# z and the mixing products of layer 0 feature-major, with upper and lower parts of the tokens in one 512-column product

## What is computed

```python
D_MODEL = 1024; SEQ = 256; D_INNER = 2048; POOL_WINDOWS = (2, 4, 8, 16)

def pool_layer(x, norm_g, w_in, w_pool, pool_scale, w_out):
    h = rms_norm(x, norm_g)
    u, z = jnp.split(h @ w_in, 2, axis=-1)
    # pool_mixer: mean over the last 2, 4, 8 or 16 tokens less u itself, by
    # group of 512 features; then per group  mixed = pooled @ w_pool[g]
    y = pool_mixer(u, w_pool, pool_scale) * jax.nn.silu(z)
    return x + y @ w_out
```

## Time and profile before

| | |
|---|---|
| median of three runs | 431.68 us |
| the profiled execution | 431.68 us, its span 429.9 us |
| TensorE busy | 423.5 us, 99% |
| VectorE, ScalarE, GpSimd busy | 281.4, 231.0, 163.1 us |
| loads | 73.8 MB read; a granule of 1 MB lands 5.0 to 5.5 us after its issue |
| granted TensorE clock | 1.00 throughout |

### The profile page before, as it was taken

How to read it: one execution, slowest core, us unless ns; L and a number is a source line. 1 busy time by engine, 2 the same in 40 slices (tenths; PEclk the granted TensorE clock), 3 DMA queues, 4 the chain that set the end, 5 groups by cost and what they waited for, 6 DMA issues and landing times.

```text
span 429.9 us, 5672 instructions
## 1 busy us (share of the span) xinstructions
PE 423.5 (99%) x2214; PEld 362.7 (84%) x2214; DVE 281.4 (65%) x340; ACT 231.0 (54%) x406; POOL 163.1 (38%) x111
## 2 busy tenths in 40 slices
PE   8999999999999999999999999999999999999997
PEld 8979898988888888888788888888888888888885
DVE  3866898688985544356664798447983579836532
ACT  5745545444554443578447765477654786546310
POOL 0077417267000000089804595055940559300000
PEclk9999999999999999999999999999999999999999
DMA  8987578645455747436833667236672355731002
GB/s 273 386 285 272 195 244 314 214 159 178 167 197 175 217 137 221 123 94 204 295 101 99 186 184 226 91 100 193 196 216 84 99 191 196 246 105 41 2 0 98
DMA packets 38026, 75.25 MB, mean 175 GB/s; under 512 B 1648, under 2 KB 1776, under 8 KB 38000
## 3 DMA queue, kind: packets, MB, share of 16 engines
q1 hardware_dynamic: 37280, 73.83, 52.8%
q10 hardware_dynamic: 720, 1.07, 0.8%
HBM read 73.84 MB, written 1.05 MB: 174 GB/s over the span
## 4 chain that ended last, share of the span: by engine, by line
PE 85%; POOL 7%; DMA 2%; DVE 2%; ACT 1%; SPq 1%; issue 1%; DVEq 0%
PE acc L599 23%; PE acc L601 22%; PE acc L600 22%; PE aux L654 4%; POOL wide L344 3%; PE acc L644 3%; PE acc L643 3%; PE acc L641 3%; DMA raw<-in_w_in_dram 2%; PE aux L738 2%; POOL k_s L337 1%; PE aux L745 1%; SPq L232 1%; PE aux L757 1%; PE aux L756 1%; PE aux L755 1%
## 5 line engine op out<-in xcount | busy, mean ns | idle before, releaser
L836 DVE TENSOR_TENSOR w_lo<-raw,w_hi 128x2048 fp32r<-128x2048 f32 x65 | 165.2, 2548 | 57.6 <-ACT w_hi L367 57.5
L367 ACT ACTIVATE w_hi<-raw 128x2048 fp32r<-128x2048 f32 x64 | 121.9, 1915 | 28.3 <-PE acc L601 21.7
L599 PE MATMUL acc<-w_hi,hT_hi 128*128 128x512 f32 x320 | 127.7, 399 | 1.0 <-DVE w_lo L836 1.0
L601 PE MATMUL acc<-w_hi,hT_lo 128*128 128x512 f32 x320 | 124.9, 390 | 0.0
L600 PE MATMUL acc<-w_lo,hT_hi 128*128 128x512 f32 x320 | 124.6, 389 | 0.0
L601 PEld LDWEIGHTS acc<-w_hi,hT_lo 128*128 128x128 f32 x320 | 60.1, 188 | 13.0
L599 PEld LDWEIGHTS acc<-w_hi,hT_hi 128*128 128x128 f32 x320 | 60.2, 188 | 12.9 <-DVE w_lo L836 1.4
L600 PEld LDWEIGHTS acc<-w_lo,hT_hi 128*128 128x128 f32 x320 | 60.2, 188 | 11.5
L599 PE MATMUL acc<-w_hi,aT_hi 128*128 128x512 f32 x160 | 63.7, 398 | 0.0
L601 PE MATMUL acc<-w_hi,aT_lo 128*128 128x512 f32 x160 | 62.4, 390 | 0.0
L600 PE MATMUL acc<-w_lo,aT_hi 128*128 128x512 f32 x160 | 62.3, 389 | 0.0
(11 more groups left out here) (125 smaller groups left out, 593.7 us busy)
## 6 DMA issues: line engine op xcount, KB each, us to landing
raw<-in_w_in_dram SPq DMA_DIRECT2D x46, 1024.0 KB, 5.5
raw<-in_w_out_dram SPq DMA_DIRECT2D x16, 1024.0 KB, 5.0
raw<-in_w_pool_dram SPq DMA_DIRECT2D x4, 1024.0 KB, 5.5
raw<-in_w_in_dram SPq DMA_DIRECT2D x8, 256.0 KB, 7.4
wide<-in_xT_dram ACTq DMA_DIRECT2D x4, 256.0 KB, 6.6
xs<-in_x_dram SPq DMA_DIRECT2D x1, 1024.0 KB, 7.7
out_dram<-ysb SPq DMA_DIRECT2D x4, 256.0 KB, 2.0
wide<-in_table_dram SPq DMA_DIRECT2D x1, 256.0 KB, 8.9
```

The lines of the kernel that those rows point to most:

```text
L367: act.activation(w_hi[:, slot, :], raw[:, slot, :], ACT.Copy).then_inc(hi_made, 1)
L599: pe.matmul(a, shi, whi, start=first and k == 0, stop=False)
L601: ins = pe.matmul(a, slo, whi, start=False, stop=last and k == GK - 1)
L836: dve.tensor_tensor(w_lo[:, slot, :], raw[:, slot, :], w_hi[:, slot, :].bitcast(F32), ALU.subtract).then_inc(w_split, 1)
```

## The change

z and the mixing products become feature-major. The upper and lower parts of the tokens lie side by side (`hT`, `aT`), so a tile of `tile_of_two` is two products: w_lo with the upper part (256 columns), then w_hi with both (512 columns). The left half of the bank then holds two of the three terms and the right half the third; all four tiles of a granule take a bank each (`quad`). ScalarE copies the right halves of two banks to SBUF, VectorE adds the left halves. For z, VectorE also multiplies by the token's factor (in the free dimension now), ScalarE takes tanh from SBUF, VectorE makes the gate. For y0, VectorE multiplies by the channel's scale and the gate, ScalarE and VectorE split the result from SBUF. The transposes of y0 are gone. Mixing granules alternate between `quad[0]` and `quad[1]`. The wait for `tables_made` moves from ScalarE to VectorE. The diff, cut to layer 0 (semaphore declarations and the shifted counts of layer 1 are left out):

```diff
@@ -98,21 +98,20 @@
-        hT_hi = sb("hT_hi", [P, KD, SEQ], F32R)
-        hT_lo = sb("hT_lo", [P, KD, SEQ], F32R)
-        aT_hi = sb("aT_hi", [P, KI, SEQ], F32R)
-        aT_lo = sb("aT_lo", [P, KI, SEQ], F32R)
+        hT = sb("hT", [P, KD, 2, SEQ], F32R)
+        aT = sb("aT", [P, KI, 2, SEQ], F32R)
...
+        rstd_half_b = sb("rstd_half_b", [P, SEQ])
+        second = sb("second", [P, 2 * SEQ])
...
+        probs_pair = sb("probs_pair", [P, 6 * P])
...
+        hT_hi, hT_lo = hT[:, :, 0, :], hT[:, :, 1, :]
+        aT_hi, aT_lo = aT[:, :, 0, :], aT[:, :, 1, :]
+        probs, probsT = probs_pair[:, 0:3 * P], probs_pair[:, 3 * P:]
+        lo_part = [t.rearrange("p (f s) -> p f s", f=2) for t in (probs_pair[:, 0:2 * SEQ], second[:, :])]
+        gateT = wide[:, :, :].rearrange("p t n -> p (t n)").rearrange("p (f s) -> p f s", f=KI)
+        y0 = [ysb[:, b].rearrange("p t n -> p (t n)").rearrange("p (f s) -> p f s", f=HPG) for b in range(2)]
...
-        acc = [[ctx.enter_context(nc.psum_tensor(f"acc{b}{t}", [P, COLS], F32)) for t in range(TT)] for b in range(2)]
-        aux = [ctx.enter_context(nc.psum_tensor(f"aux{i}", [P, COLS], F32)) for i in range(4)]
+        quad = [ctx.enter_context(nc.psum_tensor(f"quad{b}", [P, 4, COLS], F32)) for b in range(2)]
+        acc = [[quad[b][:, t, :] for t in range(TT)] for b in range(2)]
+        aux = [quad[1][:, 2, :], quad[1][:, 3, :], quad[0][:, 2, :], quad[0][:, 3, :]]
@@ -417,33 +424,43 @@
                 static_hi(4 * g + 4)
                 if g == 0:
                     act.wait_ge(rstd_spread, 1)
-                    act.activation(rstd_b[:, :], aux[2][:, 0:SEQ], ACT.Copy).then_inc(rstd_b_made, 1)
+                    act.activation(rstd_b[:, :], aux[2][:, 0:SEQ], ACT.Copy)
+                    act.activation(rstd_half_b[:, :], aux[2][:, 0:SEQ], ACT.Copy, scale=0.5).then_inc(rstd_b_made, 1)
                 if g > 0:
                     pooled_out(g - 1)
                 static_hi(4 * g + 5)
                 static_hi(4 * g + 6)
-                if g == 0:
-                    act.wait_ge(tables_made, 1)
-                for t in range(TT):
-                    product_ready(act, t, 2 * g + 1, 4 * g + 3)
-                    act.activation(wide[:, t, g * COLS:(g + 1) * COLS], acc[1][t][:, :], ACT.Tanh,
-                                   scale=rstd_half[:, t:t + 1]).then_inc(tanh_made, 1)
+                for p in range(2):
+                    product_ready(act, p, 2 * g + 1, 4 * g + 3)
+                    if g > 0:
+                        act.wait_ge(gate_made, 2 * (g - 1) + p + 1)
+                    act.activation(lo_part[p], quad[1][:, 2 * p:2 * p + 2, SEQ:], ACT.Copy).then_inc(lo_copied, 1)
+                for p in range(2):
+                    act.wait_ge(z_made, 2 * g + p + 1)
+                    act.activation(lo_part[p], gateT[:, HPG * g + 2 * p:HPG * g + 2 * p + 2, :],
+                                   ACT.Tanh).then_inc(tanh_made, 1)
                 static_hi(4 * g + 7)
             for g in range(GROUPS):
                 layer0(g)
             pooled_out(GROUPS - 1)
+            def y0_lo_part(g):
+                for p in range(2):
+                    product_ready(act, p, 8 + g, N_POOL + g)
+                    act.wait_ge(*((y0_summed, 2 * (g - 1) + p + 1) if g else (gate_made, 2 * (GROUPS - 1) + p + 1)))
+                    act.activation(lo_part[p], quad[g % 2][:, 2 * p:2 * p + 2, SEQ:], ACT.Copy).then_inc(lo_copied, 1)
+
             def y0_hi(g):
-                for b in range(2):
-                    turned_hi(aT_hi, HPG * g + 2 * b, 2 * (g % 2) + b, (y_turned, 2 * g + b + 1), y_hi, gain=2 * KD)
+                for p in range(2):
+                    act.wait_ge(y0_made, 2 * g + p + 1)
+                    f = HPG * g + 2 * p
+                    act.activation(aT_hi[:, f:f + 2, :], y0[g % 2][:, 2 * p:2 * p + 2, :], ACT.Copy).then_inc(y_hi, 1)
             for g in range(GROUPS):
-                if g > 0:
-                    static_hi(N_POOL + 3 + g)
-                    y0_hi(g - 1)
-            static_hi(N_OUT0 + 3)
-            y0_hi(GROUPS - 1)
+                y0_lo_part(g)
+                static_hi(N_POOL + 4 + g)
+                y0_hi(g)
             def h1_hi(half):
                 for t in range(TT):
@@ -646,6 +663,49 @@
                             ins.then_inc(tile0_ready, 1)
                 ins.then_inc(w_used, 1)
+            def tile_of_two(out_, n, c, h, start, stop):
+
+
+                pe.matmul(out_[:, 0:SEQ], w_lo[:, n % RING, c:c + P], h[:, 0, :], start=start, stop=False,
+                          skip_group_check=True)
+                return pe.matmul(out_, w_hi[:, n % RING, c:c + P], h.rearrange("p a s -> p (a s)"), start=False,
+                                 stop=stop, skip_group_check=True)
+
+            def z_granule(g, j):
+                n = 4 * g + 2 + j
+                if j == 0 and g > 0:
+                    pe.wait_ge(z_made, 2 * g)
+                if (g, j) == (0, 0):
+                    pe.wait_ge(half_split, 1)
+                else:
+                    pe.wait_ge(w_split, n + 1)
+                for f, k in [(f, k) for f in range(HPG) for k in range(GK)] if j else \
+                        [(f, k) for k in range(GK) for f in range(HPG)]:
+                    if (g, j, f, k) == (0, 0, 0, 2):
+                        pe.wait_ge(w_split, n + 1)
+                    if (g, j, f, k) == (0, 0, 0, 3):
+                        sum_tokens()
+                    if (g, j, f, k) == (0, 1, 2, 0):
+                        spread_rstd()
+                    ins = tile_of_two(quad[1][:, f, :], n, k * COLS + f * P, hT[:, GK * j + k], j == 0 and k == 0,
+                                      j == 1 and k == GK - 1)
+                    if j == 1 and k == GK - 1 and f == 1:
+                        ins.then_inc(tile0_ready, 1)
+                ins.then_inc(w_used, 1)
+
+            def mix(g):
+                n = N_POOL + g
+                pe.wait_ge(w_split, n + 1)
+                pe.wait_ge(pooled_split, g + 1)
+                pe.wait_ge(*((u_made, 2 * GROUPS), (z_made, 2 * GROUPS), (y0_summed, 2), (y0_summed, 4))[g])
+                for f in range(HPG):
+                    for k in range(GK):
+                        ins = tile_of_two(quad[g % 2][:, f, :], n, k * COLS + f * P, aT[:, HPG * g + k], k == 0,
+                                          k == GK - 1)
+                    if f == 1:
+                        ins.then_inc(tile0_ready, 1)
+                ins.then_inc(w_used, 1)
+
             def turn(dst_banks, src, made, tiles=range(HPG)):
                 for f in tiles:
@@ -687,40 +747,27 @@
                 if g > 0:
                     u_granule(g, 0)
                     u_granule(g, 1)
-                for j in (2, 3):
-                    granule(4 * g + j, j, 1, (gate_made, TT * g) if g else None, hT_hi, hT_lo, GK * (j % 2),
-                            first=j == 2, last=j == 3, halves=g == 0 and j == 2,
-                            mid=(sum_tokens, spread_rstd)[j - 2] if g == 0 else None, mid_at=5 - j)
+                z_granule(g, 0)
+                z_granule(g, 1)
             for g in range(GROUPS):
                 layer0(g)
-            def turn_y0(g):
-                pe.wait_ge(y0_made, g + 1)
-                if g >= 2:
-                    pe.wait_ge(y_split, 2 * (g - 1))
-                turn((2 * (g % 2), 2 * (g % 2) + 1), ysb[:, g % 2], y_turned)
-
             pe.wait_ge(ident_made, 1)
             for g in range(GROUPS):
-                free = (y0_made, g - 1) if g >= 2 else ((u_made, gate_made)[g], TT * GROUPS)
-                pe.wait_ge(pooled_split, g + 1)
-                granule(N_POOL + g, g, g % 2, free, aT_hi, aT_lo, HPG * g, first=True, last=True)
-                if g > 0:
-                    turn_y0(g - 1)
+                mix(g)
             def turn_x1(half):
                 pe.wait_ge(x1_made, TT * (half + 1))
+                pe.wait_ge(y0_summed, 2 * GROUPS)
                 turn((2 * half, 2 * half + 1), xs[:, :, half * COLS:(half + 1) * COLS], h_turned)
             for half in range(2):
                 for q in range(4):
                     pe.wait_ge(y_split, 2 * (q + 1))
-                    granule(N_OUT0 + 4 * half + q, q, half, (y0_made, 3 + half), aT_hi, aT_lo, GK * q,
+                    granule(N_OUT0 + 4 * half + q, q, half, (y0_summed, 2 * (3 + half)), aT_hi, aT_lo, GK * q,
                             first=q == 0, last=q == 3)
-                    if (half, q) == (0, 0):
-                        turn_y0(GROUPS - 1)
                     if (half, q) == (1, 0):
                         turn_x1(0)
@@ -918,12 +964,18 @@
                 if g > 0:
                     pooled_rest(g - 1)
                 weight_lo(4 * g + 6, 2)
-                for t in range(TT):
-
-                    dve.wait_ge(tanh_made, TT * g + t + 1)
-                    gate = wide[:, t, g * COLS:(g + 1) * COLS]
```

(74 more changed lines are left out.)

4 lines of the change are left out of this document (1 added, 3 removed).

## The result

The changed kernel takes 440.85 us in the median of 4 runs (440.58 to 440.92), the kernel before 431.71 (431.66 to 431.87, 4 runs). The ratio is 1.021, with a 95% interval from 1.0192 to 1.0228: slower by 9.1 us. Forecast were 440.2, in a range from 436.0 to 443.6. The profiled execution took 440.92 us, its span is 439.1, so 1.8 us lie around it, as before.

A forecast was written before the change was run, and what follows sets the result against it. TensorE's product pitch bounded the kernel before; late VectorE would delay the changed one. First output granule 133.3 - 123.6 - 0.9 = +8.8 us, taken as +8.5 for overlap: 431.7 + 8.5 = 440.2, range 436.0 to 443.6.

The forecast's parts named there:

- Products: TensorE, z and mixing granules: 16 pairs of 0.120 + 0.227 us, 5.55 for 5.44; twelve granules, +1.3 us.
- Transposes: TensorE, mixing granules: the transposes of y0 go, 0.91 us each granule, four times, 3.6 us gone.
- VectorE's stage: VectorE's queue for one layer 0 slice: 22.9 us (21.4 in slice 0), against TensorE's stage of 22.6.
- First z sums: VectorE, slices 0 to 3: at 38.4, 60.8, 83.7, 106.6; 6.1, 6.4, 6.7 us behind TensorE in slices 1 to 3.
- Wait one: TensorE before mix(1), which needs z(3) read: starts at 110.9 where it could at 105.5, 5.4 us.
- Wait two: TensorE before mix(2), which needs y0(0)'s sums: starts at 120.4 when mix(1) ends at 116.5, 3.9 us.
- The slices of y0: VectorE behind mix(2)'s start: 6.4 us a slice against 5.55 for a mixing granule; two further TensorE waits of 0.9 each.
- The end: TensorE's first output granule waits for y0(2)'s sums: starts at 133.3 against 123.59 before; +8.8 us after 0.9 for transposes.
- Rival 3: TensorE's clock falls in the waits before mix(1) and mix(2): for both adds 5.7 us, 446; chance 0.05.
- Rivals 1, 2 and 4: 1: VectorE's added work hidden, 429.3, chance 0.07; 2: no GpSimd collisions, 431.6, 0.05; 4: TensorE's weight loads exposed, 442.4, 0.05.
- GpSimd's collisions: VectorE's last z multiply waits for GpSimd's fourth window sum, taken 0.5 us longer by its row than the lock rule gives.
- the case: The forecast's own case, late VectorE making TensorE wait: spans 436.8 to 443.6 us, chance 0.78.

The follow-up runs named there:

- the kernel with all queues in order: Changed kernel, ScalarE's upper parts 4g+5 and 4g+7 moved ahead; behind slice 3, y0 sums ahead of pooling, weights and gates: 430.72 us, 0.9975 of before.
- the first experiment: Changed kernel with the upper part of weight 4g+7 ahead of the two tanh on ScalarE: 435.98 us, 1.0096 of the kernel before.
- the second experiment: Changed kernel with upper part 4g+7 ahead of the tanh and 4g+5 ahead of the pooled copy on ScalarE: 434.64 us, 1.0068 of before.

## Why the prediction was right

- **Products.** Forecast 0.347 us a pair; 32 pairs of z(1) took 55.13 - 43.82 = 11.31 us, 0.353. That is another 0.1 us for a granule that runs at that pitch. It could not be seen in the 440.85, where it went into the waits, but it is in the kernel with all queues in order: on TensorE alone the change was to give 2.4 us, and gave 1.2 (430.72 against 431.91). Seven granules at that pitch, z(1) to mix(0), are 0.7 of the missing 1.2, and a hitch at the start of mix(1) is 0.4: two pairs take 1.07 us there (105.86 to 106.93) instead of 0.70.
- **Transposes.** Gone, 3.6 us. Three of the four blocks stood where TensorE now waits and were worth nothing; the last, behind the first output granule, counts with 0.9.
- **VectorE's stage.** 22.9 us forecast, 23.1 measured. The missing 0.2 is in the walk: it took 2.3 us for the lower part behind the second idle time, where the earlier trace rows have 2.5 (93.64 - 91.13). The idle time behind the gates was to be 1.1 and is 1.11; that for the second upper part 1.7 (+12.2 to +13.9), and is 1.53. The new copies over two banks take 0.58 to 0.60 us and tanh from SBUF 0.63, so the 0.9 that widened the range upwards was not needed.
- **First z sums.** Forecast 38.4, 60.8, 83.7, 106.6; measured 38.73, 61.16, 84.22, 107.28. Over three slices the walk lost 0.7 us, 0.3 of them in its start. TensorE had z(1), z(2), z(3) ready at 55.13, 77.96 and 100.78 (where its next product starts), so VectorE was 6.0, 6.3 and 6.5 us behind; 6.1, 6.4 and 6.7 were forecast. Nearly all of this lateness comes from slice 0, and a stage as long as TensorE's never makes it up. The kernel before is late in slice 0 as well (its first gate starts at 39.21) and catches up in its idle time. Whether an earlier start in slice 0 alone would have saved the time was not tried.
- **Wait one.** Mix(1) was to start at 110.9 and started at 111.58, its wait 5.0 for 5.4 (TensorE reached it at 106.4, not 105.5, by the pitch of the pairs).
- **Wait two.** Mix(2) was to start at 120.4 and started at 121.05. The walk from z to y0's sums, 9.5 us, took 9.5. But the wait is 1.8, not 3.9, since mix(1) took 7.5 us instead of 5.55: TensorE filled the wait with slower products. The two waits of 0.9 forecast behind it, at mix(3) and the first output granule, did not come at all, because mix(2) was slow too (below). So TensorE's idle time, to rise from 6 to about 17 us, is 12.6: the time of the late queues was forecast well, its split between waiting and slow products was not.
- **The slices of y0.** 6.4 us each forecast, 6.19 and 6.18 measured. This one step was counted too long: behind the first sum the operations follow one another without handovers, a sum every 0.60 us. From mix(2) to the output granule it makes 12.9 forecast, 12.4 by the sums (131.99 - 119.62).
- **The end.** The first output granule was to start at 133.3 and did at 133.81; the sums of y0(2) were ready at 133.3 (the second at 132.59, 0.69 long).
- **Rival 3, the clock,** was right in its mechanism and small in its price: the clock did fall in both granules. The granted clock over the two mixing granules, in a view of stretches (from:to, length, busy time of PE, PEld, DVE, ACT and POOL, PEclk, DMA share, GB/s):

```profile
110.00:120.00 10.00, 7.69 (x32) 6.43 (x32) 7.64 (x9) 5.67 (x7) 0.28 (x1) 0.72 0.48 159
120.00:126.50 6.50, 5.45 (x22) 4.76 (x23) 6.50 (x11) 5.25 (x6) 0.00 (x0) 0.74 0.17 42
126.50:134.00 7.50, 7.50 (x44) 6.61 (x43) 7.50 (x13) 4.05 (x5) 0.00 (x0) 1.00 0.61 204
```

In mix(1) six pairs ran at 0.64 us instead of 0.35, with the granted clock at 0.50 (1.2 GHz) from 111.5 to 115.6, then the full level came back; in mix(2) five pairs did, from 122.54 on, with 0.50 again up to 125.8. Mix(1)'s loss of 1.95 us lay in wait two. Mix(2) took 7.2 us, so mix(3) began at 128.26 where the sums were done at 127.1, and of this some 0.4 us is left at the output granule, 133.81 against 133.3 and the 0.15 us that mix(2) had between its sum's end (120.90) and its start. The prediction bounded it by whole granules at half rate, 5.7; it was 0.4, since the level returned after 4.0 and 3.2 us. The single run of the other order in the pair bears this out: there mix(2) ran at the full level and the time was 440.37, 0.5 less. The Trainium skill, page TensorE: Matmul & The Clock Gate, section HAM oscillation, has an idle array throttled to half its rate. This trace agrees for mix(1): behind its wait the granted clock was 0.50. In mix(2) the level fell 1.5 us after the work had begun again.
- **Rivals 1, 2 and 4.** 1 and 2 needed a late VectorE to be hidden, and no cover was there. 4 was to cost 13.4 us on TensorE; the pairs ran 0.1 us a granule over the sum, and whether even that is the weight load's was not shown.
- **GpSimd's collisions.** The multiply was to wait for the fourth window sum, which I took 0.5 longer by its row. GpSimd in order of time:

```profile
98.53 3.82 POOL L313 TENSOR_TENSOR qkT<-ysb 128x1024 f32<-128x1024 f32 x1
...
105.28 4.27 POOL L313 TENSOR_TENSOR qkT<-ysb 128x1024 f32<-128x1024 f32 x1
```

The second of these took 4.27 us, and the multiply 2.12 instead of 0.69. The choice of the row over the rule of the Trainium skill was right in size, though the row does not say why. A sum of this size takes 1.89 us alone, so it began its work at about 107.66, 0.3 after the weight's lower part ended at 107.35, while VectorE ran a sum with a PSUM operand (an estimate, from the row's end less 1.89). The rule of the lock (the Trainium skill, page SBUF — State Buffer, section SBUF: two separate sides) fits the multiply, which has two SBUF inputs and waited; the 0.3 it does not explain, and that stays open.

The first output granule came 0.5 us later than forecast (133.81 for 133.3). The clock (+0.4) and the pace of the y0 slices (-0.5) cancelled, which was luck; the late start of mix(1) (+0.7) is what is left there, within 0.1. The sum had also taken off 0.3 us, in case dependent operations on VectorE overlap. They hardly do: a multiply starts 0.71 us after its sum (84.93 - 84.22), where operations in a row are 0.61 apart. The 0.5 and the 0.3 make up the step from 440.2 to 440.85, 0.65, within 0.2.

Two slips of the prediction changed nothing. It names one wait of TensorE on a product in the kernel before; there is a second, of 0.6 us at 7.09, on the upper part of u's first weight. And its range adds 1.7 and another 1.7 us downwards and 1.4, 1.1 and 1.0 upwards, which gives 443.7 for the upper end, and leaves GpSimd's 1.0 out of the lower end of the case.

## What to carry to other kernels

TensorE's 99% said nothing of how late its neighbours could be. Before work is put on an engine that is busy 65%, walk one stage of its queue in order, with every wait that its order makes, and set the sum against the stage of the bound engine: here 22.9 against 22.6, after an idle wait of 1.1 us behind another engine's queue had been opened. Look at the first stage by itself as well: the excess of a stage was small, and 6 us of lateness came in with slice 0 and stayed. And where a change takes work from TensorE and gives it to others, write each queue again in the order in which its results are due; here the gain (1.2 us) came only then. Move first what other engines wait for; it costs no work and was worth 10 us here.

## What the runs showed of the hardware beyond the forecast

- **A short wait can cost TensorE's clock afterwards.** Behind 5.0 us of waiting six pairs ran at 1.2 GHz (granted clock 0.50), from the first on. Behind a wait of 1.8 us (after that earlier one) the level fell 1.5 us into the work, for five pairs. With two waits of 1.43 and 2.49 us, in the first experiment, five wide products took 0.63 us, from 117.45 on; with one wait of 2.4 us, in the second, none did. The same view of stretches in the first experiment, from the second wait on:

```profile
116.10:120.00 3.90, 3.88 (x15) 3.37 (x16) 3.90 (x6) 3.23 (x6) 0.00 (x0) 0.65 0.00 0
120.00:124.00 4.00, 4.00 (x22) 3.48 (x22) 4.00 (x9) 1.85 (x3) 0.00 (x0) 0.92 0.80 253
```

- **Two paces of the same pair.** It runs at 0.353 us in z(1) to mix(0) and at 0.347 in mix(1), once the clock is back, and in mix(3). In the kernel with all queues in order too, the pace goes from 0.353 to 0.347 at mix(1), after a hitch of 0.4 us. But not every hitch or wait does this: in the second experiment the pace stayed at 0.354 behind the same hitch of 0.4 us at mix(1) and a wait of 2.4 at mix(2), and went to 0.347 only behind the wait of 0.3 at mix(3). So the same kind of granule runs at either pace, and the order of the pair does not decide. The cause was not found.
- **A load does not show between unlike products.** The weight load is 0.19 us long, the narrow product 0.12 behind it, and both paces lie within 0.006 us of the sum of the two widths' own.
